# A six-layer transformer stack on one core: the down products of the MLPs begin with whole tiles in order instead of two interleaved tiles

## The reference

```python
D_MODEL = 1024
D_FF = 4 * D_MODEL
...
def sq_relu_mlp(h, w_up, w_down):
    u = jnp.einsum('btd,df->btf', h, w_up)
    return jnp.einsum('btf,fd->btd', jnp.square(jax.nn.relu(u)), w_down)
...
        h = h + sq_relu_mlp(rms_norm_2(h, mlp_norm_g[layer]), mlp_w_up[layer], mlp_w_down[layer])
```

## Time and profile before

| | before |
|---|---|
| median of 3 runs | 1832.25 us (1831.91 to 1832.4) |
| profiled execution | 1835.86 us |
| its span, first to last instruction | 1834.0 us |
| TensorE busy (products) | 1789.8 us, 98% |
| VectorE, ScalarE, GpSimd busy | 1150.3, 866.9, 450.9 us |
| mean granted TensorE clock | 0.995 |
| DMA | 149.20 MB, mean 81 GB/s |

### The profile page before, as it was taken

The page is one execution under the profiler, slowest core; times in us unless marked ns, Lnnn a source line. Parts: engine busy times, 40 slices in busy tenths (PEclk is TensorE's granted clock), DMA queues, the critical chain, the costliest instruction groups (busy, mean ns, idle before and its releaser), DMA issues.

```text
span 1834.0 us, 26208 instructions
## 1 busy us (share of the span) xinstructions
PE 1789.8 (98%) x10340; PEld 1460.4 (80%) x10340; DVE 1150.3 (63%) x1861; ACT 866.9 (47%) x1409; POOL 450.9 (25%) x451
## 2 busy tenths in 40 slices
PE   7999999999999999999999999999999999999997
PEld 6877777775678757677879898988888787989896
DVE  5355556575546688854578575765677657858574
ACT  5236665455435465564345252633445434435253
POOL 0035551101311235560140000005678214000000
PEclk9999999999999999999999999999999999999999
DMA  5321111231013411111232322222222123232322
GB/s 177 101 78 49 47 47 58 80 101 50 24 47 100 133 60 34 36 36 58 80 122 86 115 93 104 93 97 83 84 88 76 46 81 127 81 115 92 106 91 80
DMA packets 44521, 149.20 MB, mean 81 GB/s; under 512 B 6000, under 2 KB 6384, under 8 KB 44400
## 3 DMA queue, kind: packets, MB, share of 16 engines
q1 hardware_dynamic: 44400, 147.53, 24.1%
HBM read 139.64 MB, written 2.10 MB: 77 GB/s over the span
## 4 chain that ended last, share of the span: by engine, by line
PE 85%; DVE 6%; ACT 4%; POOL 2%; issue 2%; DMA 1%; POOLq 0%; SPq 0%; DVEq 0%; ACTq 0%
PE BANK L301 18%; PE BANK L303 17%; PE BANK L302 17%; PE BANK L2405 4%; PE BANK L2404 4%; PE BANK L2402 4%; PE BANK L955 3%; PE BANK L688 2%; PE BANK L1739 1%; PE BANK L1720 1%; DMA WRAW<-in_wc 1%; DVE WL L278 1%; PE BANK L1696 1%; PE BANK L1012 1%; PE BANK L2710 1%
## 5 line engine op out<-in xcount | busy, mean ns | idle before, releaser
L269 ACT ACTIVATE WH<-WRAW 128x1024 fp32r<-128x1024 f32 (+1 forms) x214 | 223.0, 1044 | 340.8 <-PE BANK L303 306.0
L278 DVE TENSOR_TENSOR WL<-WRAW,WH 128x1024 fp32r<-128x1024 f32 (+1 forms) x201 | 256.3, 1276 | 138.8 <-ACT WH L269 138.6
L301 PE MATMUL BANK<-HH,WH 128*128 128x512 f32 x664 | 273.1, 411 | 12.1 <-DVE WL L278 9.8
L303 PE MATMUL BANK<-HL,WH 128*128 128x512 f32 x664 | 260.2, 392 | 0.0
L302 PE MATMUL BANK<-HH,WL 128*128 128x512 f32 x664 | 259.9, 391 | 0.0
L301 PE MATMUL BANK<-HIDH,WH 128*128 128x512 f32 (+1 forms) x520 | 201.2, 387 | 1.6 <-issue 1.5
L302 PE MATMUL BANK<-HIDH,WL 128*128 128x512 f32 (+1 forms) x520 | 200.7, 386 | 0.0
L303 PE MATMUL BANK<-HIDL,WH 128*128 128x512 f32 (+1 forms) x520 | 200.7, 386 | 0.0
L2405 PE MATMUL BANK<-HP,G 128*128 128x256 f32 x672 | 190.2, 283 | 0.0
L2404 PE MATMUL BANK<-HP,G 128*128 128x256 f32 x672 | 190.2, 283 | 0.0
L2402 PE MATMUL BANK<-HP,G 128*128 128x256 f32 x672 | 190.1, 283 | 0.0
(11 more groups left out here) (446 smaller groups left out, 3694.2 us busy)
## 6 DMA issues: line engine op xcount, KB each, us to landing
WRAW<-in_w SPq DMA_DIRECT2D x77, 512.0 KB, 3.5
WRAW<-in_wd SPq DMA_DIRECT2D x64, 512.0 KB, 3.5
RAW<-in_wf SPq DMA_DIRECT2D x32, 512.0 KB, 3.6
WRAW<-in_wu SPq DMA_DIRECT2D x16, 512.0 KB, 3.5
TMP<-in_wf SPq DMA_DIRECT2D x16, 512.0 KB, 3.5
WRAW<-in_w0o SPq DMA_DIRECT2D x8, 512.0 KB, 3.5
WRAW<-in_w1o SPq DMA_DIRECT2D x8, 512.0 KB, 3.4
WRAW<-in_wc SPq DMA_DIRECT2D x8, 512.0 KB, 3.5
```

Source lines behind the costliest of these rows:

```text
L269: e.activation(WH[b % NS][:, 0:n], WRAW[b % NR][:, 0:n], ACT.Copy).then_inc(*inc("s_high", ("high", b)))
L278: e.tensor_tensor(WL[b % NS][:, 0:n], WRAW[b % NR][:, 0:n], WH[b % NS][:, 0:n].bitcast(F32), ALU.subtract).then_inc(*inc("s_low_pool" if p ...
L301: e.matmul(dst, ah, bh, start=first and i == 0, stop=False)
L303: made = e.matmul(dst, ah, bl, start=False, stop=last and i == len(sets) - 1)
```

## The change

TensorE now issues all eight steps of tile 0, then all eight of tile 1, and so on, in each of the four down stages of each of the two MLPs:

```diff
                 ks = (0, 4, 1, 5, 2, 6, 3, 7) if c else tuple(range(8))
                 banks.i = 0
-                for m in range(2):
-                    down(c, m, ks[0:6])
-                for m in range(2):
-                    down(c, m, ks[6:8])
-                for m in range(2, 7 if L and c == 3 else 8):
+                for m in range(7 if L and c == 3 else 8):
                     down(c, m, ks)
```

## The result

| | before | after |
|---|---|---|
| median | 1832.08 us (1831.8 to 1832.4, 4 runs) | 1858.05 us (1857.59 to 1858.53, 4 runs) |
| ratio | | 1.0142, 95% interval 1.0124 to 1.0159 |
| profiled execution | 1835.86 us | 1857.59 us |
| its span | 1834.0 us | 1855.8 us |

What follows compares the result with a forecast made beforehand. TensorE, busy 1789.8 of 1834.0 us, was taken as the bound. Stops of 19.8 us plus clock falls of 9.6 made 29.4 us, taking the median 1832.25 to 1861.6 us; range 1851 to 1867.

Steps and rivals of the forecast that it cites:

- the chains don't move: Down stages: the work making the last hidden parts waits for no down product, so keeps its time against stage start.
- chunk 0, each MLP: First down stage: TensorE stops 4.27 us for hidden tile 7's low part, so tile 2 starts 3.36 us later.
- chunks 1 to 3, six stages: TensorE stops about 2.05 us per down stage for the last hidden pair; with restarts 13.1 us over six stages.
- one fall: TensorE's clock drops to half for 3.4 us after a stop, costing 1.6 us.
- falls behind the short stops: Chunks 1 to 3: four of the six stops of about 2.05 us bring a half-clock stretch, 1.6 us each.
- five to seven more stretches at half clock: Sign expected in the profile after the change: this many additional half-clock periods on TensorE.
- main case: Whole kernel: 1858.5 (two long, two short falls) to 1866.5 us (eight and one double), chance 0.50.
- the clock holds at the short stops: Rival: clock falls at the two long stops or at none, 1852 to 1855.3 us, chance 0.36.
- Later waits that swallow the delay: Rival: idle time later in the MLPs absorbs the stops, so hardly anything is lost; chance 0.04.
- The change that doesn't do what it says: Rival: the moved steps are not where intended in TensorE's order; time 1832 us, chance 0.02.
- More than counted: Rival: double-length falls at most stops, or a chain of weights turning late; 1868 to 1872 us, chance 0.06.
- Planes in time: Rival: hidden parts arrive early enough, no new stops, chunk 0's 0.75 us waits go; 1830.7 us, chance 0.02.

Runs made afterwards that it cites:

- experiment 4: The changed kernel with TensorE's stops filled by thrown-away products, 8 in chunks 1 to 3 and 17 in chunk 0: 1851.97 us.
- experiment 3: The changed kernel with three steps of tile 1 put ahead of the last two of tile 0 in every down stage: 1836.17 us, ratio 1.0018.
- 5: The changed kernel with VectorE making relu and square of the last hidden pair in one operation in chunks 1 to 3: 1850.07 us.
- 7: The changed kernel with chunk 0's last hidden tile made earlier by two moves, on ScalarE and GpSimd: 1849.15 us.
- 6: The kernel before, with chunk 0's first two tiles interleaved as seven steps and one instead of six and two: 1830.81 us, ratio 0.9991.
- 8: The kernel before, interleaved, with chunk 0's high weight part and last hidden low part made earlier on ScalarE and GpSimd: 1830.05 us, ratio 0.9986.
- experiments 2: The kernel before with whole tiles in chunks 1 to 3 alone, chunk 0 keeping the interleaving: 1846.88 us.

## Why the prediction was right

| step of the prediction | forecast | measured |
|---|---|---|
| the chains don't move | 9.06 and 6.05 us into the stage | 8.98 and 6.03 |
| chunk 0, each MLP | 3.36 | 3.39 (experiment 4, without falls) |
| chunks 1 to 3, six stages | 13.1 | 13.2 (2.16 + 2.17 + 2.17 + 2.20 + 2.14 + 2.34) |
| stops together | 19.8 | 20.0 |
| one fall | 1.6 | 1.3 to 1.7 single, 2.4 to 2.8 double |
| falls behind the long stops | 2 | 2, one of them double: 4.3 us |
| falls behind the short stops | 4 of 6 | 1 of 6: 1.6 us |
| sum | 29.4 | 25.9 (medians: 26.0) |

The mechanism and every stop came as worked out: from start to start TensorE is held up 4.23 us at the long stops (4.27 forecast) and 2.06 at the short ones (2.05). The last hidden parts are late for whole tiles, nothing later swallows the delay, no other stop stands in the stages, so block 4's weights are not late, and the sum leaves nothing that earlier freeing of tile 0's slot could have given. The term that was mis-sized is the clock: "both long stops and four of the six short ones, 6 x 1.6 = 9.6". The runs showed one of six, and the long stops cost more than the single price because one of them brought a double fall; 5.9 in place of 9.6. The two errors partly cancel (4.8 us too much for the short stops, 1.1 too little for the long ones), and that is luck. The sign "five to seven more stretches at half clock" was missed: the profile has three in the down stages. I had reasoned that 2.05 us is longer than any stop that fell in the trace of before. But the falls there came among small products of 128 columns and fewer, a setting that isn't that of the down products; the row that was nearest in kind, 1.55 us between wide products without a fall, pointed the other way, and I gave it too little weight. The measured 1858.05 lies in the range, 0.4 us below the lower end of my main case (1858.5) and 2.8 above the upper end of the rival "the clock holds at the short stops" (1855.3), which would have been met but for one fall and one double length.

The Trainium skill (TensorE: Matmul & The Clock Gate, "Why this matters for your kernels") would have kept the falls to the gaps of over about 3 us. The runs agree that such gaps, between products of the down stages, bring one always (14 of 14), and show that shorter ones are not free of it (5 of 24 at 1.9 to 2.1 us). Of the good loop nest that the Trainium skill shows (same page, "Loop structure matters more than you think") the runs show the limit: it presumes that all steps of the tile have their operands. Here the last ones don't, and three steps of another tile ahead of them are worth 22.6 us (26.0 - 3.4, experiment 3).

The other rivals fell as follows. Later waits that swallow the delay: the growth of the eight stages, 25.9 us, arrives in full in the medians, 26.0. The change that doesn't do what it says: the stops stand where it puts them. More than counted, 1868 and up: one double fall, and no weights late. Planes in time: they are not, and where they are made earlier the loss shrinks with them (5 and 7). The gain of 1.5 us in the 0.75 stops is real but has nothing to do with whole tiles; it is had on top of the interleaving (6 and 8).

What I did not try: holding the falls fixed while changing the stops. Which of the short stops brings a fall can't be told from these runs; in both profiles of the change it is the one in chunk 2 of the first MLP, in experiments 2 and 7 others.

## What to carry to other kernels

When tiles are summed over operands that arrive one after another, count the work that stands ahead of the last operand against the time at which it arrives, stage by stage; interleaving two accumulations costs nothing here and hides six steps of the other tile, 4.1 us. Price a stop of TensorE twice, for itself and for the half clock behind it, and take the second from stops among the same kind of products. Where a fix is wanted, look at what else the producing engines do ahead of the late operand: two moves on ScalarE and GpSimd took the stop of 0.75 us out of chunk 0 of the kernel before, and left 0.9 of the 4.1 us in the changed one.

## What was not expected of the hardware

A fall of the clock is not bound to one length: behind the same stop of 4.1 us, 3.4 us (costing 1.3 to 1.5) or 6.8 us (2.4 to 2.8) at the lower level came. Nor does it begin where TensorE goes on again. Windows of the changed kernel in the stop that ends at 1543.79 and behind the one that ends at 1105.00:

```profile
1539.80:1543.10 3.30, 0.00 (x0) 0.00 (x0) 0.99 (x2) 2.75 (x4) 3.14 (x4) 1.00 0.51 159
1543.13:1543.79 0.66, 0.00 (x1) 0.03 (x1) 0.66 (x1) 0.66 (x1) 0.66 (x2) 0.50 0.00 0
...
1105.00:1106.20 1.20, 1.20 (x5) 1.02 (x6) 0.00 (x0) 0.00 (x0) 0.00 (x0) 1.00 0.00 0
```

The first fell while TensorE still stood, 0.66 us before it went on, the second 1.2 us after it had gone on. Over the 19 falls of the down stages in the profiles, the five double ones began 0.66 to 1.55 us before TensorE went on, the 14 single ones from 0.34 before to 1.32 after. While TensorE stands still a low clock can't cost it anything, and the cheapest double fall (2.4 us) is the one that began 1.55 us before the end of its stop.

Yet the four timed runs of the change lie within 0.94 us of each other. And products that are thrown away are a means against a fall: filling the stops took 6.1 us off the change while the stops ended within 0.1 us of where they had.
